# Feed-forward input of a hybrid encoder step: the seventh block product in PSUM bank 7, the adaLN columns beside the adaLN rows in bank 5, and a wait for its own last reader at every bank

## The reference

```python
def swiglu(h, w_in, w_out):
    gate, up = jnp.split(h @ w_in, 2, axis=-1)
    return (jax.nn.silu(gate) * up) @ w_out

def ada_params(c, w_ada, b_ada):
    mod = jax.nn.silu(c) @ w_ada + b_ada
    return mod.reshape(c.shape[0], N_ADA, D_MODEL)

def trunk_layer(x, c, mixer, w_ada, b_ada, g_norm, w_ffn1_in, w_ffn1_out, w_out, w_ffn2_in, w_ffn2_out):
    mod = ada_params(c, w_ada, b_ada)
    x = residual(x, swiglu(modulate(x, g_norm[0], mod[:, 0], mod[:, 1]), w_ffn1_in, w_ffn1_out), g_norm[1], mod[:, 2], 0.5)
    heads, new_state = mixer(modulate(x, g_norm[2], mod[:, 3], mod[:, 4]))
    x = residual(x, heads @ w_out, g_norm[3], mod[:, 5], 1.0)
    x = residual(x, swiglu(modulate(x, g_norm[4], mod[:, 6], mod[:, 7]), w_ffn2_in, w_ffn2_out), g_norm[5], mod[:, 8], 0.5)
```

## Time and profile before

| | us |
|---|---|
| median of 3 runs | 1413.08 |
| lowest and highest run | 1409.79, 1415.2 |
| the profiled execution | 1412.4 |
| its span, first to last instruction | 1410.6 |
| PE busy in the span (share) | 1299.4 (92%) |
| DVE busy | 825.4 (59%) |
| ACT busy | 572.7 (41%) |
| POOL busy | 319.1 (23%) |
| mean granted clock of PE (share of full) | 0.964 |

### The profile page before, as it was taken

The page is one execution under the profiler, slowest core; times in us unless marked ns, Lnnn a source line. Parts: engine busy times, 40 slices in busy tenths (PEclk is TensorE's granted clock), DMA queues, the critical chain, the costliest instruction groups (busy, mean ns, idle before and its releaser), DMA issues.

```text
span 1410.6 us, 23706 instructions
## 1 busy us (share of the span) xinstructions
PE 1299.4 (92%) x8072; PEld 1137.0 (81%) x8072; DVE 825.4 (59%) x1445; ACT 572.7 (41%) x1131; POOL 319.1 (23%) x276
## 2 busy tenths in 40 slices
PE   4999999999999977999997678959999999999996
PEld 2889999999778867888885356849999999988885
DVE  2666667676435455334337964348777777754545
ACT  4543434343334355322113464355344434434433
POOL 0443434333100000000011513005344444510000
PEclk9999999999999997999989598989999999999998
DMA  9544545454432421311321432112322332222242
GB/s 317 171 150 149 157 142 161 142 156 128 163 127 81 143 79 50 130 60 60 127 69 37 136 111 76 31 74 60 90 75 73 89 89 78 71 67 74 90 134 112
DMA packets 167003, 152.71 MB, mean 108 GB/s; under 512 B 10361, under 2 KB 139777, under 8 KB 166954
## 3 DMA queue, kind: packets, MB, share of 16 engines
q1 hardware_dynamic: 165610, 148.24, 33.5%
q0 software_dynamic: 1344, 3.81, 0.9%
HBM read 142.72 MB, written 9.05 MB: 108 GB/s over the span
## 4 chain that ended last, share of the span: by engine, by line
PE 80%; DVE 10%; issue 4%; ACT 4%; DMA 2%; DVEq 0%; POOL 0%; SPq 0%; ACTq 0%; POOLq 0%
PE ps L1083 77%; DVE resid L1961 1%; DVE h_sums_lo L1742 1%; DVE w_sums_lo L1742 1%; DVE max_den L2250 1%; DMA resid<-in_x_sample 1%; DMA w_raw<-in_w_ffn_in 1%; DVE w_lo L1742 1%; DVE act_t L1853 1%; DVE probs L2259 1%; DVE silu_gate L1846 1%; ACT x_norm L660 1%; PE ps L1125 1%; DVE y L1924 0%; ACT modulated_pairs L711 0%
## 5 line engine op out<-in xcount | busy, mean ns | idle before, releaser
L1083 PE MATMUL ps<-h_sums_hi,w_sums_hi 128*128 128x320 f32 x1216 | 378.8, 316 | 14.7 <-ACT silu_gate L730 4.7
L1083 PE MATMUL ps<-h_sums_hi,w_sums_lo 128*128 128x320 f32 x1216 | 371.4, 310 | 0.0
L1083 PE MATMUL ps<-h_sums_lo,w_sums_hi 128*128 128x320 f32 x1216 | 371.3, 310 | 0.0
L1083 PEld LDWEIGHTS ps<-h_sums_hi,w_sums_hi 128*128 128x128 f32 x1216 | 227.6, 188 | 31.4 <-issue 20.4
L1742 DVE TENSOR_TENSOR w_lo<-w_raw,w_hi 128x512 fp32r<-128x512 f32 (+3 forms) x106 | 100.0, 944 | 229.2 <-ACT w_hi L804 154.6
L1083 PEld LDWEIGHTS ps<-h_sums_lo,w_sums_hi 128*128 128x128 f32 x1216 | 228.0, 189 | 0.0
L1083 PEld LDWEIGHTS ps<-h_sums_hi,w_sums_lo 128*128 128x128 f32 x1216 | 227.8, 188 | 0.0
L1083 PE MATMUL ps<-w_hi,act_hi 128*128 128x512 f32 x440 | 173.4, 394 | 3.6 <-issue 3.6
L1083 PE MATMUL ps<-w_lo,act_hi 128*128 128x512 f32 x440 | 171.4, 390 | 0.0
L1083 PE MATMUL ps<-w_hi,act_lo 128*128 128x512 f32 x440 | 171.4, 390 | 0.0
L1742 DVE TENSOR_TENSOR w_sums_lo<-w_raw,w_sums_hi 128x512 fp32r<-128x512 f32 x136 | 126.2, 933 | 54.4 <-ACT w_sums_hi L748 44.6
(11 more groups left out here) (325 smaller groups left out, 1872.4 us busy)
## 6 DMA issues: line engine op xcount, KB each, us to landing
w_raw<-in_w_ffn_in SPq DMA_DIRECT2D x88, 512.0 KB, 3.8
w_raw<-in_w_ada SPq DMA_DIRECT2D x28, 1024.0 KB, 5.1
w_raw<-in_w_ffn_out SPq DMA_DIRECT2D x88, 256.0 KB, 2.6
w_raw<-in_w_in SPq DMA_DIRECT2D x10, 1024.0 KB, 5.1
w_raw_start<-in_w_ada SPq DMA_DIRECT2D x8, 1024.0 KB, 7.9
w_raw<-in_w_out SPq DMA_DIRECT2D x4, 1024.0 KB, 5.0
k_cache<-in_cache_k SPq DMA_DIRECT2D x8, 512.0 KB, 4.9
v_cache<-in_cache_v SPq DMA_DIRECT2D x8, 512.0 KB, 3.6
```

The lines of the kernel that those rows point to most:

```text
L1083: return pe.matmul(out, lhsT, rhs, start=start, stop=stop)
```

## The change

Product 6 goes to bank 7 instead of bank 1, so that each bank but bank 4 has one product and one reader in a turn. The adaLN columns, which were in bank 7, go into bank 5 behind the 256 columns of the adaLN rows. The waits follow: `ada_mm` waits for the bias add of the columns before (which `ada_tr` waited for), since both now use bank 5; ahead of products 1, 3, 4, 5 and 6 PE waits for the add of the turn before that reads the product's own bank last (adds 2, 3, 5, 6 and 7), and product 2 needs none, since add 1 stands ahead of add 2. In the output stage the tiles 1 to 4 wait for adds 2, 1, 3 and 5 of the last turn, instead of add 7 for tile 1 and the last activation product for tile 2.

```diff
--- before.py
+++ after.py
@@ -439,7 +439,7 @@
         ORDER = (0, 1, 5, 3, 4, 2, 6)
         LO_ORDER = (0, 1, 5, 3, 4, 6)
 
-        PRODUCTS = [(0, 0, 0), (3, 5, 1), (4, 4, 2), (1, 1, 3), (5, 3, 4), (2, 6, 6), (6, 2, 1)]
+        PRODUCTS = [(0, 0, 0), (3, 5, 1), (4, 4, 2), (1, 1, 3), (5, 3, 4), (2, 6, 6), (6, 2, 7)]
 
         PLAIN = ((0, 1, 3, 2), (4, 5, 6, 2))
 
@@ -1102,14 +1102,14 @@
 
                 pe.wait_ge(a_landed, 16 * (n + 1))
                 pe.wait_ge(a_row, n)
+                pe.wait_ge(a_mod, n)
                 ada_strips(lambda strip: PS[strip, 5, 0:ADA_COLS], unit_view(RAW[:, 1, :])).then_inc(a_mm, 1)
 
             def ada_tr(n):
 
                 pe.wait_ge(a_row, n + 1)
-                pe.wait_ge(a_mod, n)
                 for j in range(2):
-                    q = mm(PS[:, 7, j * NB:(j + 1) * NB], AROW[:, 1, j * P:(j + 1) * P], CON[:, CS18:CS18 + NB])
+                    q = mm(PS[:, 5, ADA_COLS + j * NB:ADA_COLS + (j + 1) * NB], AROW[:, 1, j * P:(j + 1) * P], CON[:, CS18:CS18 + NB])
                 q.then_inc(a_tr, 1)
 
             def norm(p, product):
@@ -1220,17 +1220,17 @@
                 if first and ada:
                     ada_tr(1)
                 if not first:
-                    pe.wait_ge(f_up, 7 * r)
+                    pe.wait_ge(f_up, 7 * r - 5)
                 product(1, f, r, first)
                 if first:
                     pe.wait_ge(f_act, r + 2 * (f + 1))
                 product(2, f, r, first)
                 if ada:
                     ada_mm(r + 2)
-                for j in (3, 4, 5):
-                    product(j, f, r, first)
-                pe.wait_ge(f_up, 7 * r + 2)
-                product(6, f, r)
+                for j, read in ((3, 4), (4, 2), (5, 1), (6, 0)):
+                    if not first:
+                        pe.wait_ge(f_up, 7 * r - read)
+                    product(j, f, r, first and j < 6)
                 if ada:
                     ada_tr(r + 2)
 
@@ -1268,10 +1268,8 @@
                             pe.wait_ge(y_copied, 4 * NT * f + t + 1)
                         elif t == 0:
                             pe.wait_ge(f_cp, (f + 1) * REG)
-                        elif t == 1:
-                            pe.wait_ge(f_up, 7 * (f + 1) * REG)
-                        elif t == 2:
-                            pe.wait_ge(f_act, (f + 1) * FT)
+                        else:
+                            pe.wait_ge(f_up, 7 * (f + 1) * REG - (5, 6, 4, 2)[t - 1])
 
                     def with_ada(n, start=False):
 
@@ -1764,7 +1762,7 @@
             def ada_mod(n):
 
                 dve.wait_ge(a_tr, n + 1)
-                add_bias(2 * ADA_FIRST + n, PS[:, 7, 0:2 * NB]).then_inc(a_mod, 1)
+                add_bias(2 * ADA_FIRST + n, PS[:, 5, ADA_COLS:ADA_COLS + 2 * NB]).then_inc(a_mod, 1)
 
             def gain(g):
                 return GT[:, g * KT:(g + 1) * KT].rearrange("p (k b) -> p k b", b=1).to_broadcast([P, KT, NB])
@@ -1875,7 +1873,7 @@
                 if weights:
                     weight_lo(3, f, r + 1)
                 ffn_act(m, f, r, 0)
-                add_product(SIL[:, HALF:TOK], 1, U4, f, r, 7, 4)
+                add_product(SIL[:, HALF:TOK], 7, U4, f, r, 7, 4)
                 if weights:
                     weight_lo(4, f, r + 1)
                     weight_lo(2, f, r + 1)
```

## The result

The median after is 1419.08 us against 1414.82 us for the kernel before, with ten runs of each. The ratio, estimated over all these runs and not from the two medians (those give 1.0030), is 1.0042, 95% interval 1.0023 to 1.0060, so 3 to 8 us slower. The forecast was 8.4 us faster.

What follows compares the result with a forecast made beforehand. TensorE was taken as all but full in both feed-forward input stages, stalling at product 1 in the second. Gain 8.9 - 0.5 = 8.4 us, so 1413.1 - 8.4 = 1404.7 us; range 1402 to 1410.

Steps and rivals of the forecast that it cites:

- The stall at product 1: Second input stage: product 1's wait for add 7 loses 0.47 us a turn, 19 times; removing it gains at most 8.9 us.
- The order turns over: Second input stage: in the third turn split 1 goes between sums 1 and 2, shortening the weight loop; 0.5 us booked.
- The first rival: Second input stage: order stays, the weight loop takes the wait over; turns 12.55 us, gain 4.4 us, time 1408.7; chance 0.25.
- Activation product 0 held by sum 4: Second input stage, vector engine: it ends about 0.35 us after sum 4; gain at worst 6.8 us.
- the other side: Second input stage: sum 4 doesn't hold activation product 0; the weight loop is 11.62 us, the gain 8.9 us.
- loop of 12.42: Second input stage: weight loop through loads, sums and splits, if sum 4 holds activation product 0: 7.08 + 4.06 + 1.28 us.
- load 4.06 us: Second input stage: time from split 2's end to sum 1's start, read from the turn shown and kept in the new loop.
- slower rival: Products 3, 4, 5: satisfied added waits stop weight loads ahead, costing 11.4 us against 8.9; time 1415.6; chance 0.07.
- The added waits at 0: Products 3, 4, 5, three more waits in each of 38 turns: taken as 0, bounded above by 11.4 us.
- adaLN in bank 5: Moved wait for the bias add, before the adaLN row product: cost 0, with 1.59 us to spare in the tightest turn read.
- the output's first waits: Output stage, tiles 1 and 2: the old waits for add 7 and the last activation product were already over; 0.
- The stall isn't add 7's: Second input stage: the time could be the loop's registers and branch, so nothing changes: 1413.1 us; chance 0.06.

Runs made afterwards that it cites:

- part 1 later: Changed kernel with activation product 1 ahead of split 2 in the second input stage, so part 1's load is issued later: 1415.63 us, ratio 1.0036.
- after_sums_f1: Changed kernel, second input stage only: GpSimd's sums reordered, split 2 ahead of split 5, activation product 0 behind both: 1407.38 us, ratio 0.9948.
- half_part0: Changed kernel, but in the second input stage part 0's load moves 256 KB instead of 512 KB: one time of 1405.03 us.
- the moves of the other loop alone: Kernel before, second input stage: GpSimd's sums reordered, split 2 ahead of split 5, activation product 0 behind both: 1416.12 us, ratio 1.0014.
- split1_after_sum2: Changed kernel, but in the second input stage split 1 waits until GpSimd has done sums 1 and 2: 1424.06 us, ratio 1.0089.

## Why the prediction was wrong, point by point

- **The stall at product 1 is add 7's, and goes.** Right: TensorE's 19 waits for silu_gate are gone in after, the first turns are 12.25, 12.40 and 12.32 us (forecast 12.31), and the old wait put back gives 12.75 again. Its worth, 8.9 us at most in the sum, was 7.5 where nothing took its place.
- **The order turns over.** Right: split 1 goes ahead of sum 2 in the third turn, as the prediction worked out, and that is what draws split 2 towards sum 4. Two turns on it's ahead of sum 1 too and holds that one instead of sum 2, with the same 6.41 us for the four sums. The first rival (the order stays) didn't come.
- **Activation product 0 held by sum 4.** Right on the side that takes it as held: split 2 ends 1.96 us behind sum 4, forecast 1.95. The product ends 0.35 us after the sum, and takes 0.48 away from it. This is the rule of the Trainium skill (SBUF — State Buffer, "Who interferes with whom") that the prediction weighed, and after agrees with it: 1.57 us against the sum. The forecast's sum, however, went by the other side: it booked the whole 8.9 us, where its own loop of 12.42 us leaves 6.8.
- **The step that failed: "load 4.06 us" in the loop of 12.42.** It was taken as fixed from the earlier trace rows, where the loads are 2.54 us apart. The same working makes split 2 end 1.95 us after sum 4 instead of 2.55, so the forecast itself moved part 1's issue towards part 0, and then kept the old landing. It measured 4.98, so the prediction had 0.92 us a turn too little, and 12.42 + 0.92 = 13.34 against 13.37. Split 4, which the prediction gave slack, is then what product 2 waits for. Half of part 0, with the issues unmoved, gives 4.03 and a turn of 12.41; part 1 later gives a shorter turn.
- **It could have been read.** The trace of before holds one such pair, ahead of its second stage's turns. Its two issues:

```profile
988.64 0.38 SPq L493 DMA_DIRECT2D w_raw<-in_w_ffn_in  x1
...
990.52 0.38 SPq L493 DMA_DIRECT2D w_raw<-in_w_ffn_in  x1
```

The second, 1.88 us behind the first, in the DMA view of before:

```profile
w_raw<-in_w_ffn_in SPq DMA_DIRECT2D x1, 512.0 KB, 4.7
```

With 1 us more for the load the loop comes to 13.4 us, and "slower" would have been the likeliest case. The prediction's slower rival was another one (the added waits).
- **The added waits at 0.** Right: with all of them in, the first input stage keeps its 261.32 us, and the turns of after_sums_f1 are 12.32 us, the 84 steps of 0.1466 us that the prediction counted.
- **adaLN in bank 5, the first stage, the output's first waits at 0.** Right for the first stage (261.32 us in both) and from the second output stage's start to the end (163.58 and 163.59 us). The first output stage has 162.27 us in before, and in half_part0 with the change in; the 164.32 us of after come with a lower clock, as said above, and stay open.
- **The other rivals.** "The stall isn't add 7's" falls with the turns of 12.25 to 12.40. "The weight loop takes the wait over" came true in kind, though in the new order and with a load that neither case had.

## What to carry to other kernels

When an edit takes a wait away, follow the loop that is late next right round to the transfers, and ask of each term whether the edit moves what that term was measured under: here the second load's distance behind the first. A duration "from issue to landing" belongs to a distance to the transfer ahead of it; read the pairs at other distances that the trace has, at a stage's edges above all. Where two limits have nearly the same length, removing one shows its worth only when the other goes too: here the change alone cost some 6 us by its ratio, the moves of the other loop alone nothing that shows, both together gained 7.

## What the hardware showed that I had not expected

- A load of 512 KB that takes 3.8 us by itself took 4.6 us when issued 1.94 us behind another of the same size on the same queue, and 3.6 when that other had 256 KB. The Trainium skill (DMA: Bandwidth & Descriptors, "Two DMAs through the same engine are not ordered") says that within one queue of one DMA engine descriptors start in order but are pipelined. The traces here don't tell the packets of the two loads apart and so don't show that order; they show the overlap in the slices of after, and these lengths.
- A later second load doesn't always end the pair later: both had landed 5.95 us after the first issue at a distance of 1.15 us, 6.54 at 1.94 and 6.3 at 2.54. In the slices of after the second transfer trails off over five slices (189 to 21 GB/s). Why 1.94 is worse than 1.15 stays open.
- In split1_after_sum2 an instruction that waited for GpSimd by a semaphore lost its place to GpSimd's own next one: sum 3 started at 1196.89 straight behind sum 2, and split 1, which waited for sum 2, at 1197.05. Sum 3 then held split 1 until 1198.73, 0.54 us past its own end.
